# Mixer layers of a four-layer fp32 transformer kernel: the last projection pair and half of the output projection move between attention units

## The chip, the cores and the metric

The kernel runs on one core of a Trainium2 chip. The metric is the device time of one execution in microseconds (us), the median over executions. All of the work is one launch: inputs are read from HBM once and one output tensor is written.

## The reference, cut to what matters

x is 512 tokens by 1024 channels, fp32. It passes a pooling layer, an attention layer, and then two layers of a second kind, each of which is a feed-forward block, a token mixer and another feed-forward block. The change touches only the two token mixers:

```python
def token_mix(h, cos, sin, w_in, sgu_w, sgu_b, w_out):
    p = h @ w_in                                   # 1024 -> 2884 columns
    u  = gelu(p[..., 0:512]); va = gelu(p[..., 512:1024])
    a_out = chunked_sgu(u, va, sgu_w, sgu_b)       # u * (tril(w_s) @ va + b), chunks of 128 tokens
    q, k = partial_rope(...), partial_rope(...)    # 8 heads of 64
    v = p[..., OFF_V:OFF_IQ]
    qi, ki, wi = ...                               # 4 index heads
    b_out = dsa_attention(q, k, v, qi, ki, wi)
    return concatenate([a_out, b_out]) @ w_out     # 1024 -> 1024

def dsa_attention(...):                            # per block of 128 queries
    score = sum_h wi[h] * relu(qi[h] @ ki.T)       # causal
    idx = top_k(score, 128)                        # the 128 best keys of each query
    p = softmax(q @ k.T * scale over idx); return p @ v
```

The first 4 chunks of 128 channels that `w_out` reads are the gated part `a_out`, the last 4 the attention part `b_out`.

## The kernel before

**Arithmetic.** Activations lie transposed, channels on the partitions, in 8 chunks of 128 x 512. Each fp32 product is three fp32r matmuls on a high and a low part of both operands (`mm3`, L1286 to L1288). Every weight slab (128 x 1024 fp32, that is 4 chunks of the inner dimension by 256 output columns) goes through the same line: SyncE loads it into one of 4 raw buffers, ScalarE copies the high part (`split_hi`, L518), VectorE subtracts for the low part (`split_lo`, L785), and TensorE uses it in 24 matmuls. There are 2 buffers for split slabs, so the high part of slab n+2 waits until TensorE is through with slab n.

**Order.** Each engine's program is written out by hand and runs in order; the engines meet through counting semaphores only. A mixer layer m (1 and 2) is `project`, `attention`, `out_phase`, on each of the four engines.

**Projection.** `A2_GROUPS` lists 12 groups: 0 index queries, 1 index key and weights (one slab), 2 and 3 q, 4 and 5 k, 6 and 7 v, 8 and 9 va, 10 and 11 u. All but group 1 have two slabs and two tiles of 128 channels. In group g VectorE splits the two slabs of group g+1 (the place of split j in group g is called slot 2g+j) and then does the post-work (`posts`) of the tiles of group g-1: the rotation of q and k, or the copy of the transposed v and va from PSUM (L979). ScalarE copies a tile out to a staging buffer only when the post-work of the tile two before it is done, and only then goes on to the next slab's high part. TensorE does the index scores (`index_scores`, two relu inputs a call) at the start and in the middle of groups 4, 5 and 6; ScalarE turns them into relus (L600), VectorE sums them (L1034).

**Top-k.** VectorE takes the 8 largest of a row (L1070) and replaces them (L1076), 16 rounds for each of the three query blocks 1, 2 and 3 (rows of 256, 384 and 512 keys); block 0 needs none. Rounds are put behind the splits by the table `ROUNDS` (L1019), from group 5 to 11. After the last one the scores become masks (L1063).

**Attention.** There are 32 units (8 heads by 4 query blocks, u from 0). On TensorE a unit is: wait for exp(u), 1 to 4 transposes of the probabilities (L1545), the scores of unit u+3 (`mm3` on 64 rows), and in every fourth unit the product with v of the head before (`values`). VectorE masks the scores (L1107) and makes the low part of the transposed probabilities (L1116), ScalarE does exp (L674) and the high part (L656). exp(0) needs the masks. In the first four heads one of the four gate products (`sgu`, L1498) is done in front of a head. v is split into high and low part in the units 0 to 3 (L669, L1127) from the copy `a_vN`. After the last head the 8 x 512 softmax denominators are spread over the partitions by matmuls with `sel` (L1565, L1566), and VectorE scales the heads (L1180) and makes h_hi and h_lo of chunks 4 to 7 (L1184).

**Output projection.** `out_phase` runs 8 slabs: for each pair of output chunks one slab with inner chunks 0 to 3 and one with 4 to 7. `residual` adds each output chunk into xT, ScalarE squares it, VectorE adds the squares for the next norm (L794, then TensorE's L1328).

Of the kernel before, what the change touches and what calls it, by code (L numbers as in the profile page):

```python
# [17 lines left out]
P = 128  # L18
S = 512
D = 1024  # L20
KC = D // P
NB = S // P
DFF = 2816
NF = DFF // P
HD = 64
# [17 lines left out]
SGU_GROUPS = 4  # L43
# [75 lines left out]
def program(nc, x, norm_mix, norm_ffn, norm_final, pool_w_in, pool_w_group, pool_scale, pool_w_out,  # L119
# [3 lines left out]
    with ExitStack() as ctx:  # L123
# [82 lines left out]
        def head_layout(prefix, n, more):  # L206

            got = layout(prefix, [("qTh", [P, n, S], FR), ("qTl", [P, n, S], FR), ("kTh", [P, n, S], FR),
                                  ("kTl", [P, n, S], FR), ("vN", [P, NB, n * P], F32)] + more)
# [6 lines left out]
            got["PTl1"] = place(prefix + "probsT_lo1", [P, PT_BLOCKS * P], FR,  # L216
                                at=reg + 4 * n * S * 4 + (0 if n == 8 else 4 * S * 4))
            return got | side

        a1 = head_layout("a1_", 8, [("masks", [P, 3, TRI[NB]], BF), ("nmx", [P, 64], F32), ("den", [P, 64], F32)])  # L220
        a2 = head_layout("a2_", 4, [
            ("iqTh", [P, 2, S], FR), ("iqTl", [P, 2, S], FR), ("ikTh", [P, 1, S], FR), ("ikTl", [P, 1, S], FR),
# [4 lines left out]
            ("m8", [P, 3, 8], F32)])  # L227
        yT = place("yT", [P, KC, S], at=reg)
# [83 lines left out]
        s_out = [sem(f"out_block{b}_stored") for b in range(NB)]  # L312

# [66 lines left out]
        def _(sp):  # L380
# [33 lines left out]
            for layer in range(2):  # L414
# [19 lines left out]
                load_list(f"out{1 + layer}", pairs_of(mix_w_out_2[layer], 0, 4), 256)  # L434
# [65 lines left out]
        def _(act):  # L500
# [86 lines left out]

            def project(m, groups, bufs):
# [15 lines left out]
                for g, (slabs, tiles) in enumerate(groups + [(0, [])]):  # L604
# [4 lines left out]
                    for j in range(slabs):  # L609
                        if m and 4 <= g <= 6:  # L610
                            relus(4 * (g - 4) + 2 * j)
                        split_hi(n + 2 + j)
                    n += slabs
                    for kind, idx in turning:
                        act.wait_ge(s_rot, RO0[m] + rotated + 1)
# [9 lines left out]
                    turning = [t for t in tiles if t[0] in ROTATED]  # L625
                    for kind, idx in tiles:
# [15 lines left out]
                        staged += 1  # L642

            def attention(m):
# [19 lines left out]
                for u in range(nu):  # L664
# [15 lines left out]
                    if m and u % 4 == 2 and u // 4 < SGU_GROUPS:  # L680
                        g = u // 4
                        act.wait_ge(s_sgu, 4 * (m - 1) + g + 1)
                        nc.scalar.activation(h_hi[:, g, :], work[:, 2 + g % 2, :], ACT.Copy).then_inc(s_hhi, 1)
                probs_hi(nu - 1)
                if m == 0:
                    act.wait_ge(s_aw, 1)
                    nc.scalar.activation(a1["fine"][:, 1], a1["fine"][:, 0], ACT.Exp).then_inc(s_ae, 1)
# [68 lines left out]
            for l in range(2):  # L756
# [3 lines left out]
                project(1 + l, A2_GROUPS, a2)  # L760
                attention(1 + l)
                out_phase(f"out{1 + l}", q + 2)
# [8 lines left out]
        def _(dve):  # L771
# [193 lines left out]
            def project(m, groups, bufs):  # L965
# [5 lines left out]
                def posts(tiles):  # L971
                    for kind, idx in tiles:
                        j = post[0]
                        post[0] += 1
                        aux = bank[4 + j % 2]
                        if kind in ("v", "va"):
# [22 lines left out]
                def take_rotated(g, tiles, first):  # L999

                    for c, (kind, idx) in enumerate(tiles):
# [10 lines left out]
                        if i >= 2:  # L1012
# [24 lines left out]
                for g, (slabs, tiles) in enumerate(groups):  # L1037
                    for j in range(slabs):
                        if m and 4 <= g <= 6:
                            index_sums(4 * (g - 4) + 2 * j)  # L1040
                        split_lo(n + 2 + j)
                        if m and g >= 5:
                            if g <= 7 and j == 0:

                                dve.wait_ge(s_idx, 12 * (m - 1) + 4 * (g - 4))
# [624 lines left out]
```

## Time and profile before

| | us |
|---|---|
| executions | 3407.11, 3406.98, 3405.28; median 3406.98 |
| the profiled execution: span | 3407.1 |
| the profiled execution: its own time | 3407.11 |
| TensorE matmul busy | 3249.5 (95%) |
| VectorE busy | 1721.4 (51%) |
| ScalarE busy | 1250.5 (37%) |
| GpSimd busy | 62.5 (2%) |

Nothing to speak of lies around the span: it starts with the first and ends with the last instruction. In the rows below, a timeline row gives start, duration, engine, line, operation, output <- inputs, and in brackets how long the engine was idle before it and who released it. x8 means that 8 like instructions are merged. PE is TensorE, DVE is VectorE, ACT is ScalarE. PEclk is the granted clock of TensorE as a share of 2.4 GHz, so that 0.50 is 1.2 GHz.

### The profile page before, as it was taken

The numbers are of one execution on the slowest core, as the hardware profiler recorded it, in microseconds if no ns is written. First come the engines' busy times: TensorE is split into PE (matmuls) and PEld (weight loads), VectorE is DVE, ScalarE is ACT, GpSimd is POOL, SyncE is SP. The second block draws the span as 40 slices with busy tenths as digits, with TensorE's granted clock in tenths as the row PEclk, the third lists the DMA queues.
The fourth block names the chain that finished last, engine by engine and source line by source line (L and its number), as shares of the span: only waits on it lengthen the run. The fifth ranks groups of instructions, "written<-read, shape, count | busy, mean of one in ns | idle before, by whom it ended". The sixth has DMA issues, their size and how long they took to land.

```text
span 3407.1 us, 39390 instructions
## 1 busy us (share of the span) xinstructions
PE 3249.5 (95%) x14426; PEld 2633.0 (77%) x14426; DVE 1721.4 (51%) x2652; ACT 1250.5 (37%) x1750; POOL 62.5 (2%) x90
## 2 busy tenths in 40 slices
PE   7899999998999999999988999999999998899998
PEld 5788888766788878888766688887888776678887
DVE  6555426555655256543776465434332568543324
ACT  3343323364434234332323344323442332444421
POOL 0000000000000000000000000000000000000000
PEclk8899999989999999999996899999999999899999
DMA  3365333201455316532321245322333322023321
GB/s 110 93 197 189 94 99 95 92 5 54 144 179 166 97 64 197 184 104 93 90 62 31 68 155 194 122 93 87 97 94 99 91 75 68 7 81 98 98 93 68
DMA packets 262762, 351.61 MB, mean 103 GB/s; under 512 B 16392, under 2 KB 208136, under 8 KB 262664
## 3 DMA queue, kind: packets, MB, share of 16 engines
q1 hardware_dynamic: 240768, 270.57, 25.5%
q0 software_dynamic: 21216, 79.30, 7.1%
q8 instruction: 62, 1.02, 0.1%
q10 hardware_dynamic: 680, 0.43, 0.0%
q14 instruction: 36, 0.29, 0.0%
HBM read 349.87 MB, written 2.10 MB: 103 GB/s over the span
## 4 chain that ended last, share of the span: by engine, by line
PE 84%; DVE 10%; ACT 3%; issue 2%; DMA 0%; SPq 0%; ACTq 0%; DVEq 0%
PE bank L1286 27%; PE bank L1288 26%; PE bank L1287 26%; DVE w_lo L785 2%; PE bank L1545 1%; DVE a_score L1076 1%; DVE a_m L1070 1%; ACT w_hi L518 1%; PE bank L1354 1%; DVE sumsq L794 1%; ACT probs L674 1%; DVE work L823 1%; DVE h_lo L829 1%; PE bank L1328 0%; DVE bank L1107 0%
## 5 line engine op out<-in xcount | busy, mean ns | idle before, releaser
L785 DVE TENSOR_TENSOR w_lo<-raw,w_hi 128x1024 fp32r<-128x1024 f32 x508 | 622.2, 1225 | 1420.8 <-ACT w_hi L518 1420.4
L1286 PE MATMUL bank<-h_hi,w_hi 128*128 128x512 f32 x2928 | 1158.8, 396 | 22.4 <-DVE w_lo L785 15.7
L1287 PE MATMUL bank<-h_lo,w_hi 128*128 128x512 f32 x2928 | 1148.1, 392 | 0.0
L1288 PE MATMUL bank<-h_hi,w_lo 128*128 128x512 f32 x2928 | 1147.6, 392 | 0.0
L518 ACT ACTIVATE w_hi<-raw 128x1024 fp32r<-128x1024 f32 x508 | 537.4, 1060 | 1447.9 <-PE bank L1288 1443.9
L1286 PEld LDWEIGHTS bank<-h_hi,w_hi 128*128 128x128 f32 x2928 | 555.7, 190 | 149.2 <-issue 31.0
L1288 PEld LDWEIGHTS bank<-h_hi,w_lo 128*128 128x128 f32 x2928 | 554.7, 189 | 118.3
L1287 PEld LDWEIGHTS bank<-h_lo,w_hi 128*128 128x128 f32 x2928 | 556.0, 190 | 114.0
L1286 PE MATMUL bank<-act_hi,w_hi 128*128 (+1 forms) x1120 | 440.9, 394 | 0.0
L1288 PE MATMUL bank<-act_hi,w_lo 128*128 (+1 forms) x1120 | 439.2, 392 | 0.0
L1287 PE MATMUL bank<-act_lo,w_hi 128*128 (+1 forms) x1120 | 434.9, 388 | 0.0
L1288 PEld LDWEIGHTS bank<-act_hi,w_lo 128*128 128x128 f32 x1120 | 210.3, 188 | 48.8
L1287 PEld LDWEIGHTS bank<-act_lo,w_hi 128*128 128x128 f32 x1120 | 210.2, 188 | 47.2
L1286 PEld LDWEIGHTS bank<-act_hi,w_hi 128*128 128x128 f32 x1120 | 210.5, 188 | 42.1
L851 DVE SCALAR_TENSOR_TENSOR ada_acc<-ada_w,cact,ada_acc 128x512 f32<-128x512 f32 x252 | 189.3, 751 | 7.7
L567 ACT ACTIVATE act_hi<-work 128x512 f32 x132 | 82.1, 634 | 131.0 <-DVE work L868 131.0
L1107 DVE CUSTOM_DVE_ANT_0 bank<-bank,a_masks 128x128 f32<-128x128 f32 (+3 forms) x128 | 63.6, 499 | 100.0 <-PE bank L1288 99.9
L1545 PE MATMUL bank<-squares,probs 128*128 128x128 f32 x320 | 70.0, 322 | 33.5 <-ACT probs L674 29.2
L871 DVE TENSOR_TENSOR act_lo<-work,act_hi 128x512 f32 x132 | 87.1, 693 | 21.2 <-ACT act_hi L567 21.2
L518 ACT ACT_TABLE_LOAD x67 | 86.0, 1283 | 8.3 <-issue 7.2
L1545 PEld LDWEIGHTS bank<-squares,probs 128*128 128x128 f32 x320 | 38.8, 157 | 62.8 <-ACT probs L674 41.4
L453 POOL DMA_DIRECT2D ada_w<-in_ada_w_dram x72 | 54.3, 754 | 1698.8 <-DVE ada_acc L851 1053.8
(195 smaller groups left out, 2337.9 us busy)
## 6 DMA issues: line engine op xcount, KB each, us to landing
raw<-in_ffn_w_in_dram SPq DMA_DIRECT2D x176, 512.0 KB, 3.5
ada_w<-in_ada_w_dram POOLq DMA_DIRECT2D x72, 1024.0 KB, 5.6
raw<-in_ffn_w_out_dram SPq DMA_DIRECT2D x88, 512.0 KB, 3.6
raw<-in_ffn_w_gate_dram SPq DMA_DIRECT2D x44, 512.0 KB, 3.9
raw<-in_ffn_w_up_dram SPq DMA_DIRECT2D x44, 512.0 KB, 3.8
raw<-in_ffn_w_down_dram SPq DMA_DIRECT2D x44, 512.0 KB, 3.7
raw<-in_mix_w_in_dram SPq DMA_DIRECT2D x44, 512.0 KB, 3.6
raw<-in_attn_w_qkv_dram SPq DMA_DIRECT2D x24, 512.0 KB, 3.5
```

The source lines that it names most:

```text
L453: pool.dma_start(ada_w[:, half], w[:, 4 * half:4 * half + 4, bass.ds(i * 512 + (f % 2) * N_MOD * 512, 512)])\
L518: nc.scalar.activation(w_hi[:, nb % SPL, :], raw[:, nb % RAW, :], ACT.Copy).then_inc(s_hi, 1)
L567: nc.scalar.activation(act_hi[:, bass.ds(i * 2 + c, 1), :], work[:, 2 + c:3 + c, :], ACT.Copy).then_inc(s_ahi, 1)
L674: nc.scalar.activation(b_["P"][:, u % 2, 0:n], bank[SCORE_BANKS[u % 3]][:, 0:n], ACT.Exp, scale=-1.0, bias=b_["nmx"][:, u:u + 1], accum_ou ...
L785: V.tensor_tensor(w_lo[:, nb % SPL, :], raw[:, nb % RAW, :], w_hi[:, nb % SPL, :].bitcast(F32), ALU.subtract).then_inc(s_lo, 1)
L851: ins = V.scalar_tensor_tensor(out=ada_acc[:], in0=w, scalar=cact[:, k:k + 1], in1=ada_acc[:], op0=ALU.mult, op1=ALU.add)
L871: V.tensor_tensor(act_lo[:, bass.ds(i * 2 + c, 1), :], work[:, 2 + c:3 + c, :], act_hi[:, bass.ds(i * 2 + c, 1), :].bitcast(F32), ALU.subt ...
L1107: V.tensor_tensor_reduce(out=scores, in0=scores, in1=bufs["masks"][:, g, TRI[b]:TRI[b + 1]], scale=-(HD ** -0.5), scalar=3e38, op0=ALU.add ...
L1286: T.matmul(dst, wh, mh, start=first, stop=False)
L1287: T.matmul(dst, wh, ml, start=False, stop=False)
L1288: return T.matmul(dst, wl, mh, start=False, stop=last)
L1545: ins = T.transpose(bank[2 + u % 2][:, k * P:(k + 1) * P], bufs["P"][:, u % 2, k * P:(k + 1) * P], ident)
```

## The change

In each of the two mixer layers:

- The last projection group (u channels 2 and 3, 2 slabs) is taken out of `project`. Its 16 steps (`last_u`, one step is one `mm3` on 128 x 512) run two at a time in front of the transposes of units 0 to 7.
- The slabs of `w_out` are loaded in another order: first the four with inner chunks 0 to 3, then the four with inner chunks 4 to 7. The first four run as 32 steps (`first_part`), two in front of the transposes of each of the units 16 to 31, into banks 5 and 7; VectorE adds each result to xT (`add_part`). The last four run after attention (`out_rest`).
- The gate products move from the heads' starts to units 9 to 12. ScalarE's Gelu of u 2 and 3 stands in unit 8, behind a slab's high part.
- Index scores start in the middle of group 3, with the three waits (L1453 to L1455 of before) that stood at group 4; top-k rounds run from slot 12 to slot 21, so that all of them end in group 10.
- v is split into high and low part directly from PSUM (`vNh`, `vNl`); the copy `a_vN` and the split in units 0 to 3 fall away. The products with v use bank 4 only.

The diff, cut to its core:

```diff
-                two = [((2, 3), 2)]
-                ROUNDS = {5: ([((1,), 1)], [((1,), 1)]), 6: ([((1,), 2)], [((1,), 3)]),
-                          7: ([((1,), 4)], [((1, 2, 3), 1), ((1,), 4)]),
-                          8: (two, two), 9: (two, two), 10: (two, two), 11: (two, [((2, 3), 1)])}
+                ROUNDS = {12: [((1,), 2)], 13: [((1,), 2)], 14: [((1, 2, 3), 1)], 15: [((1, 2, 3), 1)],
+                          16: [((1, 2, 3), 2)], 17: [((1, 2, 3), 2)], 18: [((1, 2, 3), 2)], 19: [((1, 2, 3), 2)],
+                          20: [((1, 2, 3), 2)], 21: [((2, 3), 4)]}
...
+        FILL = {u: ("u", 2 * u) for u in range(8)} | {u: ("out", 2 * (u - 16)) for u in range(16, 32)}
...
-                load_list(f"out{1 + layer}", pairs_of(mix_w_out_2[layer], 0, 4), 256)
+                by_pair = pairs_of(mix_w_out_2[layer], 0, 4)
+                load_list(f"out{1 + layer}", by_pair[0::2] + by_pair[1::2], 256)
...
@@ TensorE, project @@
                     if m and 4 <= g <= 6:
-                        if g == 4:
-                            pe.wait_ge(s_post, PO0[m] + 3)
-                            pe.wait_ge(s_wi, m)
-                            pe.wait_ge(s_wT, m)
-                        index_scores(4 * (g - 4))
-                        between = 4 * (g - 4) + 2
+                        index_scores(2 * (2 * g - 7))
+                    if m and 3 <= g <= 5:
+                        between = 2 * (2 * g - 6)
...
+                                if between == 0:
+                                    pe.wait_ge(s_post, PO0[m] + 3)
+                                    pe.wait_ge(s_wi, m)
+                                    pe.wait_ge(s_wT, m)
                                 index_scores(between)
@@ TensorE, mix (in place of attention) @@
+                pe.wait_ge(s_post, PO0[m] + 19)
+                pe.wait_ge(s_actT, AT0[f"out{m}"] - 2)
...
+                for u in range(nu):
+                    if u in FILL:
+                        what, step = FILL[u]
+                        for s in (step, step + 1):
+                            last_u(s) if what == "u" else first_part(s)
+                    pe.wait_ge(s_exp, u0 + u + 1)
+                    if u >= 2:
+                        pe.wait_ge(s_pt, u0 + u - 1)
+                    for k in range(u % 4 + 1):
+                        ins = T.transpose(bank[2 + u % 2][:, k * P:(k + 1) * P], bufs["P"][:, u % 2, k * P:(k + 1) * P], ident)
+                    ins.then_inc(s_tr, 1)
+                    if u + 3 < nu:
+                        scores(u + 3)
+                    if 9 <= u < 13:
+                        sgu(u - 9)
+                    if u % 4 == 1 and u >= 5:
+                        values(u // 4 - 1)
+                values(nh - 1)
...
@@ ScalarE, mix @@
+                    if u:
+                        probs_hi(u - 1)
+                    if u % 4 == 2 and u >= 4:
+                        o_out(u // 4 - 1)
+                    if u == 4:
+                        split_hi(out)
+                    if u == 8:
+                        split_hi(out + 1)
+                        for idx in (2, 3):
+                            act.wait_ge(s_used, nb + 2)
+                            nc.scalar.activation(b_["uT"][:, idx, :], bank[3 + 2 * (idx - 1)][:], ACT.Gelu).then_inc(s_actT, 1)
+                    if 10 <= u < 14:
+                        g = u - 10
+                        act.wait_ge(s_sgu, 4 * (m - 1) + g + 1)
+                        nc.scalar.activation(h_hi[:, g, :], work[:, 2 + g % 2, :], ACT.Copy).then_inc(s_hhi, 1)
+                    if u in (20, 24, 28):
+                        split_hi(out + (u - 20) // 4 + 2)
...
@@ VectorE, mix @@
+                    if u == 5:
+                        split_lo(out)
+                    if u == 9:
+                        split_lo(out + 1)
+                    if 11 <= u < 15:
+                        sgu_lo(m, u - 11)
+                    if 9 <= u < 13:
+                        sgu(m, bufs, u - 9)
+                    if u >= 18 and u % 2 == 0:
+                        add_part((u - 18) // 2)
+                    if u in (21, 25, 29):
+                        split_lo(out + (u - 21) // 4 + 2)
...
+                add_part(7)
...
@@ TensorE, out_rest @@
+                    for c in range(2):
+                        for j in range(4):
+                            if i == 0 and c == 0:
+                                pe.wait_ge(s_hlo, H0[f"attn{m}"] + 4 + j + 1)
+                            ins = mm3(bank[2 * (i % 2) + c][:], hi[:, j, c * P:(c + 1) * P], lo[:, j, c * P:(c + 1) * P],
+                                      h_hi[:, 4 + j, :], h_lo[:, 4 + j, :], j == 0, j == 3)
+                        if c == 0:
+                            ins.then_inc(s_even, 1)
+                    ins.then_inc(s_used, 1)
```

## Rows read from the trace of the kernel before

**Rows 1.** The page, part 4: the chain that ended last, by engine

```profile
PE 84%; DVE 10%; ACT 3%; issue 2%; DMA 0%; SPq 0%; ACTq 0%; DVEq 0%
```

**Rows 2.** Stretches; busy of PE, PEld, DVE, ACT, POOL, then PEclk, DMA, GB/s

```profile
1751.50:1821.50 70.00, 55.08 (x235) 42.88 (x233) 62.70 (x144) 17.21 (x22) 0.00 (x0) 0.90 0.25 76
1821.50:1909.40 87.90, 78.49 (x300) 52.91 (x300) 43.00 (x119) 40.13 (x114) 1.51 (x2) 0.66 0.04 13
1909.40:1955.00 45.60, 45.60 (x193) 37.56 (x193) 17.64 (x22) 12.49 (x15) 0.00 (x0) 0.95 0.32 101
2891.90:2967.40 75.50, 64.43 (x300) 43.55 (x300) 42.55 (x117) 40.11 (x114) 0.00 (x0) 0.82 0.00 1
```

**Rows 3.** Stretches of 4 us in attention, first and second mixer layer

```profile
1842.00:1846.00 4.00, 4.00 (x15) 2.93 (x14) 2.19 (x5) 1.23 (x5) 0.00 (x0) 0.50 0.00 0
2914.00:2918.00 4.00, 4.00 (x25) 2.77 (x24) 2.80 (x9) 1.52 (x5) 0.00 (x0) 1.00 0.01 2
```

**Rows 4.** VectorE timeline, first layer, projection and top-k

```profile
1684.43 0.67 DVE L1057 TENSOR_TENSOR a_wT<-bank,squares 128x512 f32<-128x512 f32 x1
...
1729.92 0.74 DVE L1034 SCALAR_TENSOR_TENSOR a_score<-work,a_wi,a_causal 128x512 f32<-128x512 f32 x1
...
1732.57 0.42 DVE L1070 MAX8 a_m<-a_score 128x8 f32<-128x256 f32 x1
...
1744.31 0.69 DVE L988 TENSOR_TENSOR turned<-bank,cos 128x512 f32<-128x512 f32 x1
...
1751.51 1.23 DVE L785 TENSOR_TENSOR w_lo<-raw,w_hi 128x1024 fp32r<-128x1024 f32 x1 [1.67 <-ACT w_hi L518]
...
1757.73 1.48 DVE L1070 MAX8 a_m<-a_score 128x8 f32<-128x256 f32 x3
...
1760.81 0.43 DVE L1070 MAX8 a_m<-a_score 128x8 f32<-128x256 f32 x1
...
1768.84 1.15 DVE L1070 MAX8 a_m<-a_score 128x8 f32<-128x384 f32 x2
...
1771.21 1.15 DVE L1070 MAX8 a_m<-a_score 128x8 f32<-128x384 f32 x2
...
1820.59 0.90 DVE L1063 TENSOR_SCALAR a_masks<-a_score 128x256 bf16<-128x256 f32 x3
```

**Rows 5.** TensorE waits in the projection, first layer: us, times, longest us

```profile
PE bank L1286 <- ACT work L600: 6.0, 3, 2.6
```

**Rows 6.** ScalarE timeline at the start of attention, first layer

```profile
1812.22 1.06 ACT L630 ACTIVATE a_uT<-bank 128x512 f32<-128x512 f32 x2
...
1813.83 1.28 ACT L674 ACT_TABLE_LOAD   x1
```

**Rows 7.** TensorE timeline, first layer, then (29xx us) second

```profile
1681.94 0.39 PE L1286 MATMUL bank<-h_hi,w_hi 128*128 128x512 f32 x1
...
1841.51 1.11 PE L1545 MATMUL bank<-squares,probs 128*128 128x128 f32 x4 [0.27 <-ACT probs L674]
...
1854.40 0.66 PE L1545 MATMUL bank<-squares,probs 128*128 128x128 f32 x4 [1.10 <-ACT probs L674]
...
1855.80 2.07 PE L1498 MATMUL bank<-a_wT,a_vaN 128*128 128x128 f32 x8
...
1900.53 0.69 PE L1286 MATMUL bank<-probsT_hi,h_hi 128*64 128x512 f32 x1 [1.41 <-DVE a_probsT_lo L1116]
...
1909.39 0.80 PE L1286 MATMUL bank<-h_hi,w_hi 128*128 128x512 f32 x1
...
1916.93 0.39 PE L1286 MATMUL bank<-h_hi,w_hi 128*128 128x512 f32 x1
...
1958.67 1.05 PE L1328 MATMUL bank<-ones,sumsq 128*128 128x1 f32 x8 [2.43 <-DVE sumsq L794]
...
2943.08 0.66 PE L1545 MATMUL bank<-squares,probs 128*128 128x128 f32 x4 [0.46 <-ACT probs L674]
...
2950.07 0.66 PE L1545 MATMUL bank<-squares,probs 128*128 128x128 f32 x4 [0.59 <-ACT probs L674]
```

More of the change, by code:

```diff
@@ L609, in project @@
                     for j in range(slabs):
-                        if m and 4 <= g <= 6:
-                            relus(4 * (g - 4) + 2 * j)
+                        if m and 7 <= 2 * g + j <= 12:
+                            relus(2 * (2 * g + j - 7))
                         split_hi(n + 2 + j)
@@ L624, in project @@
                         rotated += 1
-                    turning = [t for t in tiles if t[0] in ROTATED]
+                    turning = [t for t in tiles if t[0] in ROTATED or (m and t[0] == "v")]
                     for kind, idx in tiles:
@@ L975, in posts @@
                         aux = bank[4 + j % 2]
+                        if m and kind == "v":
+                            dve.wait_ge(s_vh, V0[m] + idx + 1)
+                            v = slice(idx * P, (idx + 1) * P)
+                            V.tensor_tensor(bufs["vNl"][:, :, v], aux[:].rearrange("p (b d) -> p b d", d=P),
+                                            bufs["vNh"][:, :, v].bitcast(F32), ALU.subtract).then_inc(s_post, 1)
+                            continue
                         if kind in ("v", "va"):
@@ L1038, in project @@
                     for j in range(slabs):
[L1039 to L1040 removed]
+                        slot = 2 * g + j
+                        if m and 7 <= slot <= 12:
+                            index_sums(2 * (slot - 7))
                         split_lo(n + 2 + j)
[L1042 to L1046 removed]
+                        if m and slot == 12:
+                            dve.wait_ge(s_idx, 12 * m)
+                        if m and slot >= 12:
+                            for blocks, rounds in ROUNDS[slot]:
                                 for _ in range(rounds):
@@ new lines, in out_rest @@
+            def out_rest(name, q_next, gate):
+                nb, e = N0[name], 8 * (int(name[3:]) - 1) + 4
+                split_lo(nb + 5)
+                for j in range(4):
+                    if j < 3:
+                        split_lo(nb + 6 + j)
+                    for c in (2 * j, 2 * j + 1):
+                        if c % 2 == 0:
+                            dve.wait_ge(s_even, e + j + 1)
+                        else:
+                            dve.wait_ge(s_used, nb + 4 + j + 1)
+                        residual(c, bank[c % 4][:], gate)
+                        if c:
+                            add_square(q_next, c - 1)
+                add_square(q_next, 7)
@@ new lines, in out_rest @@
+            def out_rest(m):
+                nb, end = N0[f"out{m}"] + 4, ATT[m]["u0"] + ATT[m]["nu"]
+                pe.wait_ge(s_pt, end)
+                pe.wait_ge(s_exp, end)
+                for i in range(4):
+                    if i >= 2:
+                        pe.wait_ge(s_x, free_x[f"out{m}"] + 2 * (i - 1))
+                    hi, lo = slab(nb + i, 256)
+                    pe.wait_ge(s_lo, nb + i + 1)
+                    for c in range(2):
+                        for j in range(4):
+                            if i == 0 and c == 0:
[3 more added lines that the diff above has]
+                        if c == 0:
+                            ins.then_inc(s_even, 1)
+                    ins.then_inc(s_used, 1)
```

241 lines of the change are left out of this document (198 added, 43 removed).

## The prediction, written before the changed kernel was run

> **What bounds the kernel now.** I read the chain that ended last first: TensorE holds 84% of it, VectorE 10%, ScalarE 3%, and no DMA [rows 1]. So weights and queues are not the subject. SyncE issues the same slabs in another order in both cases, and GpSimd's transfers wait for the end of attention as before. Both engines' issues cost nothing, hidden under a DMA share of 0.25 to 0.32 in the projection. Next I cut the mixer of the first of the two layers into stretches [rows 2]. From 1751.5 to 1821.5 TensorE is busy for 55 of 70 us and VectorE for 63: the end of the projection is set by the top-k rounds. From 1821.5, when the masks are ready, to 1909.4 TensorE is busy for 78 of 88 us, but at a mean clock of 0.66. In the second layer the same work takes 75.5 us, at 0.82. The output projection follows with 45.6 us. In short stretches of attention TensorE shows 4.00 of 4.00 us busy at clock 0.50 in one layer and 4.00 of 4.00 at 1.00 in the other [rows 3]. Attention is thus TensorE work at one of two clocks, with small waits, and what the filling is worth hangs on the clock. The two layers differ by 12.4 us for that reason alone, and I cost them apart.
>
> **Term 1, the masks.** The change moves the first index scores into group 3, with a wait for wT. VectorE has wT at 1685.1 [rows 4], while TensorE would go on with the next slab at 1681.94 [rows 7]: a new wait of 3.2 us, with the two scores 3.8. TensorE's stream behind it, and so every slab up to group 6, comes that much later. The waits for relus in mid-group (6.0 us in three, the longest 2.6 in group 6 [rows 5]) stay in groups 4 and 5 and fall away in group 6. On VectorE the last rotated tiles of group 5 were done at 1729.92, now at 1732.6 (3.8 later, less 1.1 for a round no longer there). Then: two score sums 1.6, a split 1.15, two lone rounds 2.0 (one is two passes of 0.42 and a load, 0.98), a split 1.15, two rounds 2.0, and the 7.2 from the k post-work at 1744.31 to the next split at 1751.51, of which 1.67 is ScalarE's chain. Slot 14 starts at 1747.7 instead of 1751.5 [rows 4].
>
> From there all is VectorE. A round over three blocks is 3.08 us (1757.73 to 1760.81), one over two 2.37 (1768.84 to 1771.21) [rows 4]. Group 7 is 2 x (1.15 + 3.08) + 1.3 for two tiles = 9.8; groups 8 and 9 are each 2 x (1.15 + 6.16) + 1.3 = 15.9; group 10 is 1.15 + 6.16 + 1.15 + 9.48 + 1.3 = 19.2. With 3 x 1.67 between them and 0.9 for the masks this is 66.7, so the masks are ready at 1814.4 instead of 1821.5: **7.1 us earlier in each layer**. It comes from two splits and some 3 us of rounds less on VectorE. The v split from PSUM is neutral: a subtract takes the place of a copy of the same 0.69 us, and ScalarE's four extra copies lie in its idle time. TensorE now has nothing to do for about 20 us before attention, since the last u slabs are no longer there. That idle time costs nothing by itself, but attention starts at 1.2 GHz.
>
> **Term 2, from the masks to the end of the output projection.** Before: 87.9 + 45.6 = 133.5 us in the first layer, 75.5 + 45.6 = 121.1 in the second [rows 2]. After, by TensorE's work at 2.4 GHz:
> - One head of four units: 2950.07 - 2943.08 = 7.0, less waits of 0.8, is 6.2 us; eight heads are 49.6. At 1.2 GHz: 1854.40 - 1841.51 = 12.9, less a gate product of 1.9, is 11.0 [rows 7].
> - A step is an eighth of a slab: 5.44 / 8 = 0.68 us, slab time from (45.6 - 7.54) / 7 [rows 2, 7]. The u steps are 16 x 0.68 = 10.9, those of w_out 32 x 0.68 = 21.8.
> - Switching into a run of wide matmuls: between nothing and 0.1 us for each of 24 units; I take 0.05, 1.2 in all.
>
> Units 0 to 7: 12.3 (two heads, the first three scores, one product with v fewer) + 10.9 + 0.4, and the clock. Dense work after 1909.39 took some 4 us to bring it up (first slab 7.54 instead of 5.44) [rows 7], while attention alone stayed at 0.50 for long. I take twice the nearest row, 7 us at half speed, 3.4 lost. Sum 27.0. Bounds: 2.1 lost, or all of it, 23.
>
> Units 8 to 15: no filling. ScalarE does, between the high part of unit 7 and exp(9), a slab's high part 1.06, a table load 1.28, Gelu for two tiles 1.06 and the load for exp again 1.28 [rows 6]. Behind them are queued exp(9) and the high part of unit 8, and TensorE needs exp(9): it stands for about 4.0 us after 1.1 us of unit 8. The rest is two heads and four gate products (0.95 each at full clock): 15.1 + 1.4 of waits at 2.4 GHz, 27.4 at 1.2. So 21.6 or 32.5; after such a stall the nearest stretches are those of rows 3, one of each kind, so I take the middle, 27.0.
>
> Units 16 to 31 with the last product with v: 24.9 + 21.8 + 0.8, 1.7 until the clock is back, and 1.4 for the low part of unit 31, where nothing fills the wait [rows 7]. Sum 50.6. VectorE's eight additions of 0.75 and three splits lie beside this; four units take TensorE about 11.6 and VectorE under 7.
>
> The tail (coefficients, scaling) stays 5.8: 1900.53 to 1909.39 less the last product, 3.1 [rows 7]. The four slabs left are 21.8, but they begin with the chunks whose low parts are only just made, where before chunks 0 to 3 covered that: 1.2 more. Sum of all: 27.0 + 27.0 + 50.6 + 5.8 + 23.0 = 133.4, starting 0.9 before the masks are through (TensorE needs only the last v and va post-work): 132.5 after the masks.
>
> First layer: 133.5 - 132.5 + 7.1 = 8.1 gained. Second: 121.1 - 132.5 + 7.1 = 4.3 lost. At the end of each, the even output chunk is now signalled half a slab before the odd one, so one residual, square and sum of the two in the last wait (2.43 shown at 1958.67 [rows 7]) goes early: 1.3 gained, twice. **Total 6.4 us, 3407.1 - 6.4 = 3400.7**, which I round to 3400. The profiled execution is 0.1 above the median shown, so this stands against the median too.
>
> **Rivals.**
> - The clock comes back soon after the stall and stays up in units 8 to 15: 21.6 instead of 27.0, and 1.7 for the return saved, 7.1 in each layer: 3386. For it: in the second layer attention holds 1.00 by itself [rows 3], and the u steps may bring it there before the stall. Against it: the stall of 4 us.
> - Slower: attention does not come up from 1.2 GHz until the w_out steps. The 20 us of idleness and the stall put it there, the u steps are too few, and the gate products and 64-row scores don't lift it. The price is 5.5 in units 8 to 15 and 6 more in the first eight, 11.5 in each layer: 3423. It decides from about 5 us more in a layer, where the gain of the first no longer pays for the second. For it: 0.50 with TensorE fully busy [rows 3].
> - The masks come no earlier, because a relu or post-work is late on VectorE behind the new wait in group 3: 7.1 lost in each layer, 3414.
>
> The Trainium skill ("TensorE: Matmul & The Clock Gate", Part 1, The HAM clock gate) has it that the default is the low clock and that sustained matmul activity, whichever it is, releases it. By that rule the first rival's 3386 would be the result. The trace disagrees in the first layer, where full busy time stayed at 0.50 [rows 3], so it gets less than half.
>
> **Chances.** Forecast (3391 to 3409) 0.42, of which a little under half is more than 0.2% below; clock kept 0.28; clock low 0.19; masks late 0.11. What a measurement can tell from no change is about 0.2%, 6.8 us. The forecast's band gives faster 0.19, same 0.19, slower 0.04 (a miss of 5 us in a layer's stall). Faster 0.47, same 0.20, slower 0.33, with the third rival partly within its bounds. The range runs from 3380 (first rival, and a start with 2.1 lost) to 3423.
>
> **What would show it.** Masks (L1063's successor) about 7 us earlier in both layers; TensorE idle for some 20 us before attention; a wait for wT of 3 us in group 3; one stall of about 4 us in unit 9 with two table loads on ScalarE; PEclk near 1.00 in units 16 to 31 in both layers; the last u steps as the first wide matmuls of attention. The prediction is wrong if the stretch from masks to the end of the output projection leaves 125 to 140 us, or if the two layers still differ by over 8 us.

## The result, and the profile after

The changed kernel takes 3417.63 us (median of 7 executions, 3415.65 to 3419.87), the kernel before 3407.11 (7 executions, 3405.28 to 3412.81) in the same comparison. The ratio is 1.0028, 95% interval 1.0017 to 1.0039: **slower by 0.28%**, where a gain, to 3400, was forecast. The profiled execution took 3415.65, its span 3414.0. In every execution whose span and own time are both listed, the own time is 1.6 to 1.7 us longer. The profiled execution of before, with its span of 3407.1, is therefore more likely the one of 3408.77 than the one of 3407.11. So the two profiles are 6.9 us apart where the medians are 10.5 apart. Of the parts of the page, the chain that ended last has moved one point from TensorE to VectorE against [rows 1]:

```profile
PE 83%; DVE 11%; ACT 3%; issue 2%; DMA 0%; SPq 0%; ACTq 0%; DVEq 0%
```

So the subject is still TensorE's stream, and next come the waits in it. TensorE's waits in the projection of the first mixer layer, 1643 to 1795 us (total, times, longest), to be held against [rows 5]:

```profile
PE bank L1446 <- ACT work L618: 3.4, 2, 1.7
PE bank L1446 <- DVE w_lo L856: 3.4, 3, 1.4
PE bank L1446 <- DVE a_wT L1133: 3.1, 1, 3.1
```

The waits are those of the forecast: one for wT of 3.1 (forecast 3.2), two for relus left of three. What they set off is in the next view, stretches of the same layer, the last row of the second (columns as in [rows 2]; PEclk is the first number after the parentheses end):

```profile
1643.46:1682.37 38.91, 35.77 (x158) 29.06 (x159) 28.01 (x40) 16.22 (x23) 0.00 (x0) 0.98 0.26 74
1682.10:1688.90 6.80, 6.53 (x19) 5.17 (x20) 2.23 (x4) 0.66 (x2) 0.00 (x0) 0.51 0.27 80
1702.60:1706.00 3.40, 3.40 (x10) 2.64 (x9) 2.52 (x4) 0.73 (x2) 0.00 (x0) 0.52 0.24 42
1705.90:1719.60 13.70, 12.02 (x55) 9.03 (x54) 8.12 (x12) 5.12 (x8) 0.00 (x0) 1.00 0.22 70
1719.60:1723.00 3.40, 3.40 (x9) 2.63 (x8) 3.17 (x4) 1.20 (x2) 0.00 (x0) 0.51 0.13 18
1751.50:1819.30 67.80, 40.59 (x177) 32.09 (x175) 61.02 (x151) 14.38 (x20) 0.00 (x0) 0.82 0.20 62
1819.30:1928.20 108.90, 98.20 (x459) 70.69 (x458) 51.78 (x128) 48.78 (x121) 1.51 (x2) 0.91 0.11 33
1849.30:1856.10 6.80, 5.97 (x21) 4.62 (x22) 3.44 (x7) 1.88 (x7) 0.00 (x0) 0.50 0.22 63
1875.00:1920.00 45.00, 44.72 (x222) 32.65 (x220) 21.55 (x53) 19.41 (x51) 0.00 (x0) 1.00 0.11 36
1928.20:1951.50 23.30, 23.30 (x96) 18.67 (x97) 14.78 (x20) 9.19 (x12) 0.00 (x0) 0.94 0.42 140
2887.90:2996.70 108.80, 98.09 (x458) 70.52 (x457) 51.74 (x128) 48.78 (x121) 0.00 (x0) 0.91 0.08 25
```

Behind each of the three waits stands a stretch at 0.51 to 0.52, that is at 1.2 GHz, full of matmuls: 6.8 us after the wait of 3.1, 3.4 us after each of the two of 1.7. The second layer shows the same three. The kernel before had the waits of 1.7 too, two in each layer, and one of 2.6. In its first layer only the 2.6 of [rows 5] has such a stretch behind it, 1729.2 to 1736.0; in its second layer only the two of 1.7 have:

```profile
1729.20:1736.00 6.80, 6.80 (x18) 4.99 (x17) 6.45 (x13) 2.21 (x4) 0.00 (x0) 0.50 0.27 77
2766.90:2770.30 3.40, 3.40 (x11) 2.60 (x9) 3.19 (x6) 1.35 (x3) 0.00 (x0) 0.50 0.00 0
2783.90:2787.30 3.40, 3.40 (x11) 2.48 (x10) 3.29 (x6) 1.77 (x3) 0.00 (x0) 0.51 0.00 0
```

So the kernel before spends 6.8 us of groups 0 to 6 at half clock in each layer, the changed kernel 13.6.

Attention with its filling (1819.3 to 1928.2, and 2887.9 to 2996.7 in the second layer) now runs at 0.91 in both layers, where [rows 2] had 0.66 and 0.82 without the filling. The two layers have become alike: 108.9 and 108.8 us.

The timelines place the forecast's landmarks. TensorE:

```profile
1643.46 0.76 PE L1446 MATMUL bank<-h_hi,w_hi 128*128 128x512 f32 x1 [0.50 <-DVE h_lo L900]
...
1682.37 0.59 PE L1446 MATMUL bank<-a_ikTh,a_iqTh 64*128 64x256 f32 x2 [3.14 <-DVE a_wT L1133]
...
1683.32 0.79 PE L1446 MATMUL bank<-h_hi,w_hi 128*128 128x512 f32 x1
...
1818.50 0.47 PE L1446 MATMUL bank<-a_kTh,a_qTh 64*128 64x128 f32 x1 [19.53 <-DVE a_vaN L1056]
...
1844.87 0.33 PE L1739 MATMUL bank<-squares,probs 128*128 128x128 f32 x1
...
1850.13 0.69 PE L1739 MATMUL bank<-squares,probs 128*128 128x128 f32 x2 [4.04 <-ACT probs L693]
...
1928.17 0.76 PE L1446 MATMUL bank<-h_hi,w_hi 128*128 128x512 f32 x1
```

VectorE, the wT product, the split of slot 14, and the masks:

```profile
1681.56 0.67 DVE L1133 TENSOR_TENSOR a_wT<-bank,squares 128x512 f32<-128x512 f32 x1
...
1751.49 1.23 DVE L856 TENSOR_TENSOR w_lo<-raw,w_hi 128x1024 fp32r<-128x1024 f32 x1 [1.67 <-ACT w_hi L528]
...
1818.36 0.89 DVE L1139 TENSOR_SCALAR a_masks<-a_score 128x256 bf16<-128x256 f32 x3
```

ScalarE in the hole after unit 8:

```profile
1844.75 1.05 ACT L528 ACTIVATE w_hi<-raw 128x1024 fp32r<-128x1024 f32 x1
1845.82 1.28 ACT L705 ACT_TABLE_LOAD   x1
1847.11 1.08 ACT L705 ACTIVATE a_uT<-bank 128x512 f32<-128x512 f32 x2
1848.22 1.28 ACT L693 ACT_TABLE_LOAD   x1
1849.51 0.47 ACT L693 ACTIVATE probs<-bank,a_nmx 128x256 f32<-128x256 f32 x1
```

Read from the layer's first projection slab (1643.46), which takes out what the layers before it did, the two kernels and the forecast stand so:

| us after the layer's first slab | before, L1 | before, L2 | forecast | after, L1 | after, L2 |
|---|---|---|---|---|---|
| split of slot 14 | 105.2 | 104.8 | 101.3 | 108.0 | 108.3 |
| masks ready | 175.1 | 174.8 | 168.0 | 175.8 | 176.1 |
| masks to end of output projection | 133.5 | 121.6 | 132.5 | 132.2 | 132.1 |
| first slab of the next block | 319.1 | 306.8 | | 318.3 | 318.6 |

In the second layer of before the masks are ready at 2891.45; the forecast counted its 121.1 from 2891.90, 0.45 too late. The first layer gained 0.8 us, the second lost 11.8. In the profiled executions 4.1 us came back outside these two stretches, where the programs are the same, so the spans differ by 3414.0 - 3407.1 = 6.9.

### The profile page after: what moved, and what is told of

Same layout as the page of the kernel before. It is cut to its first block, busy times and chain, and to the rows that moved or that the text cites. A ratio compares the mean times of both kernels' runs of the same rounds, so it can differ in the third digit from the quotient of the medians.

```text
span 3414.0 us, 39410 instructions
## 1 busy us (share of the span) xinstructions
PE 3230.4 (95%) x14426; PEld 2618.9 (77%) x14426; DVE 1723.6 (50%) x2660; ACT 1255.1 (37%) x1754; POOL 62.4 (2%) x90
## 4 chain that ended last, share of the span: by engine, by line
PE 83%; DVE 11%; ACT 3%; issue 2%; DMA 0%; SPq 0%; ACTq 0%; DVEq 0%
PE bank L1446 27%; PE bank L1448 26%; PE bank L1447 26%; DVE w_lo L856 1%; DVE a_score L1152 1%; DVE a_m L1146 1%; ACT w_hi L528 1%; DVE sumsq L865 1%; PE bank L1514 1%; PE bank L1822 1%; PE bank L1739 1%; DVE work L894 1%; DVE h_lo L900 1%; PE bank L1488 0%; DVE rot L1066 0%
## 5 line engine op out<-in xcount | busy, mean ns | idle before, releaser
L1446 PE MATMUL bank<-a_kTh,a_qTh 64*128 64x128 f32 (+3 forms) x128 | 56.9, 445 | 39.8 <-DVE a_vaN L1056 39.1
L939 DVE TENSOR_TENSOR work<-work,bank 128x512 f32<-128x512 f32 x132 | 84.4, 680 | 0.0
```

What stands on the lines that cost most here:

```text
L939: V.tensor_tensor(work[:, 2 + c, :], work[:, c, :], bank[2 + c][:], ALU.mult).then_inc(s_dveT, 1)
L1446: T.matmul(dst, wh, mh, start=first, stop=False)
```

## The experiments

All comparisons are of medians with the kernel before, taken on the same chip. To hold an experiment against the changed kernel I take the difference of its ratio and 1.0028, times 3407 us. Each ratio has an interval of 3 to 6 us on either side, so differences of a few us are read from the landmarks in the traces instead. "Masks" is again counted from the layer's first slab.

One thing has to be known for the second layer. Three of the experiments (the Gelu, the attention at full clock, the u pair) change nothing in the groups with these three waits, and still their second layer has less time at half clock in the projection than the changed kernel: behind the same wait of 3.15 for wT stand 3.4 us at half clock, not 6.8. Their masks come there 1.8 to 2.9 us earlier. That part of their gain is not the edit's, so I give what lies behind the masks apart.

### The wT wait taken away

```diff
-                    if m and g == 2:
+                    if m and g == 1:
```

The product for wT (L1133) comes one group earlier on VectorE.

> The product wT is made one group earlier on VectorE, nothing else moves. Theory (the new wait in group 3 and the low clock behind it made the masks late): the wait of 3.1 us shrinks to about 1 us (the post-work of the index key is still awaited), the slab behind it takes 5.5 instead of about 8.5 us, and the masks come 4 to 5 us earlier in each layer; whole kernel 8 to 10 us faster than the changed kernel. Rival (VectorE alone sets the masks, by its own work): masks within 1 us of where they are, kernel the same within 2 us.

Measured 3404.17 (11 executions), ratio 0.9988 [0.9979, 0.9997]: 13.6 us less than the changed kernel. Masks at 168.9 and 169.2 in the two layers, 6.9 earlier. TensorE's waits in the projection, the same window:

```profile
PE bank L1446 <- ACT work L618: 3.4, 2, 1.7
PE bank L1446 <- DVE w_lo L856: 3.4, 3, 1.4
PE bank L1446 <- DVE a_ikTl L1070: 0.9, 1, 0.9
```

```profile
1811.74 0.89 DVE L1139 TENSOR_SCALAR a_masks<-a_score 128x256 bf16<-128x256 f32 x3
```

A wait of 3.1 became one of 0.9, 2.2 us less, and the masks gained 6.9. The two relu waits are as long as ever. Two thirds of the wait's price were thus something else. In each layer one stretch of 3.4 us at half clock is left in groups 0 to 6, so 6.8 + 3.4 us of them went, which is 5.1 lost no more: 2.2 + 5.1 = 7.3, and 6.9 came back. That the masks now come within 0.9 to 1.2 of the 168.0 of Term 1 is partly chance: the forecast had the wait of 3.2 in it. With the shorter wait it would say 165.8, and the 3.1 to 3.4 left over are mostly the stretch still at half clock (1.7) and VectorE's rounds, which take 1.1 longer than forecast (below).

### The waits kept, the clock kept too

Ahead of the three waits TensorE does matmuls whose result nobody reads. It first waits for a piece of post-work that is done shortly before the one it needs, so that they fall into the time in which it would stand.

```diff
+                                pe.wait_ge(s_post, PO0[m] + {0: 2, 4: 5, 8: 7}[between])
+                                keep_warm(24 if between == 0 else 13, 5)
                                 if between == 0:
                                     pe.wait_ge(s_post, PO0[m] + 3)
```

> Dummy matmuls stand in front of the three waits of TensorE in the projection, 24 in group 3 and 13 each in groups 4 and 5; the waits themselves stay. Theory (the clock falls behind each wait and costs 6.5 us in a layer): granted clock 1.00 from group 3 to group 6, slot 14 starts 6 us earlier counted from the first slab, the masks 5 to 6 us earlier, kernel 10 to 12 us faster than the changed kernel. Rival (the waits themselves are the loss, the clock is not): slot 14 moves less than 1 us, kernel the same or 1 us slower.

Measured 3408.66 (11 executions), ratio 1.0001 [0.9992, 1.0010]: 9.2 us less than the changed kernel. The first layer from the first of the three waits to the third:

```profile
1686.00:1720.00 34.00, 32.34 (x166) 25.29 (x165) 21.54 (x33) 11.75 (x21) 0.00 (x0) 1.00 0.23 62
```

The clock is 1.00 throughout. TensorE gets past the wait for wT no sooner (at 38.7, against 38.9 in the changed kernel), since it needs the same data, yet slab 15, counted from 0, starts at 103.9 instead of 109.4 and the masks come at 170.2 and 170.3, 5.6 and 5.8 earlier. From the index scores ahead of each relu wait to those behind it TensorE takes 8.8 us, where the changed kernel takes 8.0 and 8.2, so the waits have not become shorter. This run parts the two causes: with the waits kept, the clock behind them alone is at least 5.7 of the 7.8 us by which the masks missed the forecast in the first layer.

### The Gelu in attention without its table loads

Gelu of u channels 2 and 3 is replaced by a copy, so that part of the computation is left out. Between this copy and the exps its trace has no table load.

```diff
-                            nc.scalar.activation(b_["uT"][:, idx, :], bank[3 + 2 * (idx - 1)][:], ACT.Gelu).then_inc(s_actT, 1)
+                            nc.scalar.activation(b_["uT"][:, idx, :], bank[3 + 2 * (idx - 1)][:], ACT.Copy).then_inc(s_actT, 1)
```

> The Gelu of u 2 and 3 in unit 8 is left out (a copy stands in its place, so that channels 2 and 3 of u go without Gelu), which takes away both table loads inside attention. Theory (the stall of 4.0 us in unit 9 is ScalarE's queue, 2.6 of it table loads): the stall shrinks to 1.5 us and the clock dip behind it, 6.8 us at half, may go too: 2.5 to 6 us less in each layer, 5 to 12 in all. Rival (another wait is as late): stall unchanged in sum, kernel within 1 us.

Measured 3409.45 (11 executions), ratio 1.0003 [0.9994, 1.0012]: 8.5 us less. The first transpose of unit 9 comes 2.4 us after that of unit 8, not 5.3, and TensorE stands there for

```profile
1848.90 0.44 PE L1739 MATMUL bank<-squares,probs 128*128 128x128 f32 x2 [1.19 <-ACT probs L693]
```

1.19 us instead of 4.04. The clock still falls behind it, but for 3.4 us and not 6.8:

```profile
1844.00:1851.00 7.00, 5.81 (x31) 4.14 (x31) 4.10 (x13) 4.12 (x12) 0.00 (x0) 0.99 0.05 18
1850.80:1854.20 3.40, 3.40 (x15) 2.50 (x14) 2.12 (x3) 0.09 (x1) 0.00 (x0) 0.50 0.41 115
```

The stall is worth 2.9 us in standing in each layer. From the masks to the end of the output projection 4.0 us are gained in the first layer but only 1.0 in the second, where a stretch of 10.2 us at half clock comes later, at 2929.4. What the clock adds is thus not the same in the two layers. Of the 8.5 us, 5.0 lie behind the masks. The stall was in the forecast at its right length, so this is a cost of the change, not the error of the prediction.

### Attention started at full clock

150 unread matmuls fill the 19.5 us in which TensorE stands before attention.

```diff
+                pe.wait_ge(s_idx, 12 * m)
+                keep_warm(150, 7)
                 pe.wait_ge(s_post, PO0[m] + 19)
```

> 150 dummy matmuls of 256 columns fill TensorE's idle 19.5 us before attention. Theory (the start of attention at 1.2 GHz costs about 3.4 us in a layer): clock 1.00 at unit 0, units 0 to 7 take 23 instead of 26.4 us, kernel 6 to 7 us faster. Rival (the dummy work is too long and delays the scores): attention starts over 1 us later than the last v and va post-work, gain eaten up, kernel within 2 us.

Measured 3411.83 (11 executions), ratio 1.0013 [1.0004, 1.0022]: 5.1 us less, though the intervals of this ratio and the changed kernel's overlap. The first transposes of attention come at 178.1 instead of 180.3, those of unit 8 at 198.5 instead of 201.4: 2.9 gained at unit 8. By the end of the output projection 1.6 and 1.7 of it are left in the two layers. So "That idle time costs nothing by itself, but attention starts at 1.2 GHz" was right, and the 3.4 put down for it came to 2.9 where it was put down, in units 0 to 7.

### The u pair back in the projection

All 12 groups are in the projection again, attention has the output steps alone. This undoes the first half of the change.

```diff
-        FILL = {u: ("u", 2 * u) for u in range(8)} | {u: ("out", 2 * (u - 16)) for u in range(16, 32)}
+        FILL = {u: ("out", 2 * (u - 16)) for u in range(16, 32)}
-                        for idx in (2, 3):
-                            act.wait_ge(s_used, nb + 2)
...
-                project(1 + l, A2_GROUPS[:-1], a2)
+                project(1 + l, A2_GROUPS, a2)
```

> The last two u slabs go back into the projection, into the 19.5 us in which TensorE is idle; top-k and the w_out steps stay as changed, the Gelu leaves unit 8. Theory (TensorE's work after the masks bounds attention, so 10.9 us of it should go where TensorE is idle): masks where they are, stall of unit 9 gone (4.0 us) with the dip behind it, but units 0 to 8 now without wide matmuls and at 1.2 GHz, about 22 instead of 26.4 us; in all 6 to 12 us less in each layer, kernel 12 to 24 us faster. Rival (without wide matmuls the clock stays at 1.2 GHz until unit 16): units 0 to 15 take as long as in the changed kernel, kernel 0 to 6 us faster at most.

Measured 3396.37 (5 executions), ratio 0.9965 [0.9951, 0.9979]: **faster than both kernels**, by 21.5 us than the changed one. The masks come at 175.8 and 173.2; from them to the end of the output projection it is 124.9 and 120.7 us instead of 132.2 and 132.1, so 18.7 of the 21.5 us lie behind the masks. The work of the u pair is 10.9 us at full clock and lies beside the top-k rounds for nothing; the stall for Gelu goes with it. The clock is no better for it, which shows in three neighbouring stretches of the first layer's attention:

```profile
1823.00:1840.00 17.00, 16.32 (x49) 10.74 (x50) 8.46 (x28) 8.03 (x22) 0.00 (x0) 0.50 0.01 1
1840.10:1863.90 23.80, 18.71 (x115) 13.56 (x113) 16.60 (x39) 13.22 (x37) 0.00 (x0) 1.00 0.14 45
1864.00:1877.70 13.70, 13.70 (x38) 9.42 (x39) 3.50 (x11) 2.57 (x8) 0.00 (x0) 0.51 0.00 0
```

Full busy time at 0.51 right behind four fifths busy at 1.00. "TensorE now has nothing to do for about 20 us before attention" was in the prediction as free, and it was its warning: the change takes 10.9 us of work out of that hole and puts it where TensorE is the bound.

### All of it together, and the steps spread

The gate products go to units 0 to 3, the steps of w_out over units 7 to 31, one or two in each; wT early, the u pair in the projection, 95 unread matmuls before attention.

```diff
+        FILL = {7: (0, 1), 8: (1, 1), 9: (2, 1), 10: (3, 2), 11: (5, 1), 12: (6, 1), 13: (7, 1), 14: (8, 2), 15: (10, 1), 16: (11, 1), 17: (12, 2), 18: (14, 1), 19: (15, 1), 20: (16, 1), 21: (17, 2), 22: (19, 1), 23: (20, 1), 24: (21, 2), 25: (23, 1), 26: (24, 1), 27: (25, 1), 28: (26, 2), 29: (28, 1), 30: (29, 1), 31: (30, 2)}
...
-                    if 9 <= u < 13:
-                        sgu(m, bufs, u - 9)
+                    if u < 4:
+                        sgu(m, bufs, u)
+                pe.wait_ge(s_idx, 12 * m)
+                keep_warm(95, 7)
```

> As the kernel with u in the gap, and: wT one group earlier; 95 dummy matmuls in the idle time that is left; gate products in units 0 to 3; the 32 w_out steps spread over units 7 to 31. Theory (masks late by the wait in group 3, attention by TensorE's work and clock): masks 4 to 5 us earlier, clock near 1.00 through all units, masks to the end of the output projection about 108 to 112 us instead of 132; kernel 45 to 55 us faster than the changed one, near 3367. Rival (with fewer wide matmuls in each unit the exp chain shows and the clock falls): stretch 120 us or more, kernel 3390 or slower.

Measured 3396.06 (6 executions), ratio 0.9963 [0.9951, 0.9975], a miss of some 29 us. The masks were early, at 168.9 and 171.1, but the unread matmuls ran past them: the first scores come at 174.6 and 176.7. VectorE stands between the masks and the first masking:

```profile
1821.09 0.30 DVE L1183 CUSTOM_DVE_ANT_0 bank<-bank,a_masks 128x128 f32<-128x128 f32 x1 [6.37 <-PE bank L1447]
```

And in the middle of attention 24 us ran at half clock in spite of them. The next two runs mend the one and take the other apart.

### Fewer unread matmuls, the steps in units 16 to 31

wT early, the u pair in the projection, 40 unread matmuls; gates and steps where the changed kernel has them. Against the kernel with the u pair back in the projection:

```diff
-                    if m and g == 2:
+                    if m and g == 1:
...
+                pe.wait_ge(s_idx, 12 * m)
+                keep_warm(40, 7)
```

> The three edits that each gained, together: wT one group earlier, the last two u slabs in the idle time of the projection, 40 dummy matmuls (not 95) behind them; w_out steps two in a unit from unit 16 as in the changed kernel. If the gains add (wT 13, u in the gap 21, warm start 6 of 3417.6): 3378. If the warm start and the u slabs in the gap are worth the same thing, the clock at unit 0: 3384. Against the first: the units without wide matmuls may let the clock fall as soon as they are left to themselves, 3390.

Measured 3379.23 (4 executions), ratio 0.9906 [0.9889, 0.9923], as expected (3378). The three single gains, 13.6 + 5.1 + 21.5 = 40.2, against 41.6 measured together by the ratio (the kernel before took 3413.24 in this comparison; the plain difference of 3417.63 and 3379.23 is 38.4): they add up, within what these ratios can tell.

### Fewer unread matmuls, the steps spread

Against the kernel with all of it together:

```diff
-                keep_warm(95, 7)
+                keep_warm(40, 7)
```

> As f_best, with 40 instead of 95 dummy matmuls: the first scores no longer wait for them. Theory (f_best lost 6 us a layer to dummies that ran on past the masks, and 24 us at half clock in the middle because one wide step in a unit does not hold the clock): 6 us less in each layer than f_best, 3384, and the long stretch at 0.50 is still there; g_combo, with two steps in a unit, is the faster one by 3 us or more. Rival (the late start itself let the clock fall): the stretch at 0.50 shrinks to 10 us or less and this one is the fastest of all, below 3372.

Measured 3375.88 (4 executions), ratio 0.9896 [0.9880, 0.9913]: **the fastest**, 1.0% below the kernel before. Masks at 169.0 and 168.5, output projection done 118.3 and 117.9 us after them, instead of 132.2. The spread kernel was expected to lose to the one before it by 6 us, because its first half of attention has no dense filling; it lost nothing that can be told apart (the intervals overlap). The reason for the expectation was there, though:

```profile
1815.00:1839.00 24.00, 22.01 (x78) 16.57 (x78) 14.44 (x31) 8.92 (x25) 0.00 (x0) 0.51 0.04 11
1839.00:1905.00 66.00, 62.97 (x321) 44.81 (x321) 33.73 (x87) 32.50 (x89) 1.51 (x2) 1.00 0.12 37
```

It pays 24 us at half clock and then has 66 us at 1.00 with almost no hole.

### Steps two to a unit from unit 7 on

Against the fastest, with the splits and additions that belong to the steps moved along:

```diff
+        FILL = {7: (0, 2), 8: (2, 2), 9: (4, 2), 10: (6, 2), 11: (8, 2), 12: (10, 2), 13: (12, 2), 14: (14, 2), 15: (16, 2), 16: (18, 2), 17: (20, 2), 18: (22, 2), 19: (24, 2), 20: (26, 2), 21: (28, 2), 22: (30, 2)}
```

> As h_spread40, with the w_out steps two in a unit from unit 7 to 22 and none in the last nine. Theory (two wide steps in a unit bring the clock back, one does not): the stretch at 0.50 ends near unit 9, the units behind 22 keep 1.00 because they start there; some 4 us less a layer than h_spread40, ratio to before 0.987 (h_spread40: 0.9896). Rival (where the wide steps lie does not matter to the clock, or the last units fall back to 0.50 without them): same ratio within 0.001, or more.

Measured 3382.41 (5 executions), ratio 0.9927 [0.9913, 0.9940]. The rival held, with a ratio 0.0031 above that of the spread kernel. The low stretches are 10 us in the first layer and 24 in the second, no less in the second than with the steps spread; the last nine units are without filling, and the output projection ends at 290.1 and 295.0 (287.3 and 286.4 spread). In the second layer 2.6 us of this are in the projection already, where the masks come at 171.1 instead of 168.5.

### The fastest with the relu waits covered

```diff
+                                pe.wait_ge(s_post, PO0[m] + {0: 2, 4: 5, 8: 7}[between])
+                                keep_warm(8 if between == 0 else 13, 5)
```

> As h_spread40, with the dummy matmuls in front of the waits in groups 3, 4 and 5 (8, 13, 13). Theory (with wT early one clock dip of 3.4 us a layer is left there, and it costs 1.5 to 2): masks 1.5 us earlier a layer, ratio 0.9885. Rival (VectorE now bounds the masks): masks and ratio unchanged.

Measured 3381.18 (5 executions), ratio 0.9926 [0.9912, 0.9940]. The projection did as expected, at clock 1.00 from 1660 to 1740:

```profile
1660.00:1740.00 80.00, 78.61 (x377) 63.02 (x376) 55.02 (x81) 30.12 (x47) 0.00 (x0) 1.00 0.26 79
```

The masks came 0.9 us earlier in each layer, 168.1 and 167.6, where 1.5 was expected, and it bought nothing in the total. The ratio is even 0.0030 higher, but 3375.88 and 3381.18 were taken on different chips, where the kernel before took 3413.24 and 3407.73; the profiled spans are 3373.2 and 3374.9. With the wT wait gone, what the relu waits still cost is too small for these runs.

## Why the prediction was wrong

The forecast was faster, 3391 to 3409 with the best chance; 3417.6 came, slower.

**The step that failed is Term 1**, "the masks are ready at 1814.4 instead of 1821.5: **7.1 us earlier in each layer**". They came 0.7 and 1.3 us later than before, so 7.8 and 8.4 were missed: 16.2 of the 17.4 us by which the two layers together missed (9.4 forecast gained and 0.8 measured in the first, 3.0 forecast lost and 11.8 measured in the second). Within the term:

- "A new wait of 3.2 us": right, 3.14, as the rows for its two ends [rows 4, 7] had it.
- "TensorE's stream behind it, and so every slab up to group 6, comes that much later": this is the sentence. The 3.8 held, and the clock came on top of it. The slab behind the wait ran at 1.2 GHz. In the first layer, against before and with the 3.8 taken off, slab 7 (counted from 0), the next one, starts 3.2 later, slab 9, behind the first relu wait, 4.9, and slab 11, behind the second, 6.7. The split of slot 14 is 6.7 later than forecast, the masks 7.8. A stretch of 6.8 us at half clock and two of 3.4 lose 3.4 + 1.7 + 1.7 = 6.8. The forecast priced the clock in attention at length and in the projection not at all, though [rows 5] shows the waits, and the stretches behind some of them were there to be read in the trace of before, at 1729.2 in the first layer and at 2766.9 and 2783.9 in the second. Keeping the clock over the same waits gave 5.7 back, taking the wT wait away 6.9.
- "From there all is VectorE ... 66.7": 67.8 (1751.5 to 1819.3). The rounds were mis-sized by 1.1.

**Term 2 was right in its sum**, 132.2 and 132.1 for 132.5. Its parts, in the first layer: units 0 to 7 from 1818.50 to 1844.87, 26.4 for 27.0; units 8 to 15 to 1874.49, 29.6 for 27.0, the stall 4.04 for "about 4.0"; units 16 to 31 with the last values 48.5 for 50.6; tail 5.2 for 5.8; rest 23.3 for 23.0. Part of that is luck: 2.6 too little in units 8 to 15 and 0.3 in the rest are made up for by 0.6, 2.1 and 0.6 too much elsewhere. The middle taken between 21.6 and 32.5 for units 8 to 15 came near because the clock did both. It fell to 0.50 twice, behind the stall (1849.3 to 1856.1, above) and again 10 us after that, and was up in between:

```profile
1866.30:1873.10 6.80, 6.75 (x25) 4.85 (x26) 3.77 (x9) 3.44 (x11) 0.00 (x0) 0.50 0.01 1
```

Had it been set by either end, the forecast would have been 5 us off in each layer. The 0.05 us for each switch into wide matmuls, 1.2 in all, rests on no row, and no run isolates it. The prediction's point that the two layers must be costed apart also held: the filling makes them alike, which repairs the layer that had the low clock (0.66) and spoils the one that had 0.82.

**The end of the layer**, "1.3 gained, twice": the sum of squares is released after 1.80 us instead of 2.43 [rows 7], 0.6 gained.

```profile
1954.56 1.45 PE L1488 MATMUL bank<-ones,sumsq 128*128 128x1 f32 x8 [1.80 <-DVE sumsq L865]
```

**The rivals.** The third, masks no earlier, 3414, is the one that came. Its mechanism was only half named: no relu or post-work was late on VectorE by itself, it was TensorE's clock behind the waits in groups 3 to 5 that made them late. It had 0.11, the least of the three, as an accident on VectorE; the trace of before, where waits in dense matmuls and the half clock behind some of them can be seen, was not read for it. The first, clock kept through units 8 to 15, did not come about: 13.6 of their 29.6 us were at half clock. The second, clock low to unit 16, did not either: the clock was up from 1825.3, 6.8 us after the first scores.

The prediction summed the change as a whole, and its parts have opposite signs. With the w_out steps in attention and without the u steps the kernel is at 0.9965, even with the wT wait still in it. The u steps lose some 19 to 21 us, and the first scores, moved ahead of wT, 13.6. That Term 2 came out right hides this: it was the sum of a gain and a loss, and the prediction never costed the one without the other.

## What to carry to other kernels

- A wait on the engine that sets the time costs its length and the clock behind it. Price a new wait in dense matmuls at up to twice its length, as the wait of 3.1 cost here, and look whether its producer can go a step earlier in its own queue: one changed index here was worth 13.6 us, twice what was forecast for the whole change.
- Work that fills holes in a bound stretch is free only if it does not come out of another hole. Ask of every moved step where it lay before; if it lay under another engine's work, it was free already.
- Undo the parts of a change one by one before judging it. Here the combination of what gained, with the rest undone, is 1.0% faster than before, where the change as made is 0.28% slower.

## What the runs showed of the hardware

- **The half clock can follow a wait of 1.7 us.** Among 512-column matmuls at 1.00, each of two waits of 1.7 us was followed by 3.4 us at 0.51 to 0.52, and the wait of 3.14 by 6.8 us at 0.51. Unread matmuls in the wait kept 1.00 (34 of 34 us). A wait of this length does not always do it. With wT early the first of the two relu waits is still followed by 3.4 us at half clock, in both layers, and the second by none. In the projections of before, three of six waits are followed by it: the 2.6 but neither 1.7 in the first layer, both 1.7 but not the 2.6 in the second. And the same wait of 3.15 had only 3.4 us behind it in the second layer of three runs. What decides between these is not shown.
- **Busy time alone did not bring the clock up.** In attention, with 64-row scores and transposes, TensorE stayed at 0.51 for 24 us with 22.0 us busy (the fastest kernel, 1815 to 1839), and in the kernel before at 0.50 for 30.6 us with 28.45 busy, below. The Trainium skill ("TensorE: Matmul & The Clock Gate", Part 1, The HAM clock gate) has it that the default is the low clock and that activity releases it; the measurement differs and decides. With w_out steps between the units (1875 to 1920 of the changed kernel) it was 1.00 throughout.

```profile
1821.50:1852.10 30.60, 28.45 (x91) 19.40 (x92) 17.36 (x48) 12.67 (x38) 0.00 (x0) 0.50 0.00 0
```

- **What decides which of the two clocks attention has is open.** The kernel before had 0.66 in one layer and 0.82 in the other with the same instructions, and the fastest kernel has 24 us at half clock while its neighbour with two steps a unit has 10 in one layer and 24 in the other. No run here isolates the cause. That wide matmuls between narrow ones help is argued from the stretches, not shown: the spread kernel gets no less of the low clock than the others and is the fastest all the same.
